# Causal mask by a matmul in PSUM and softmax normalisation by diagonal matrices in a two-block network on one core

## What is computed

```python
# MLA, 8 heads of 128+64: causal over blocks of 128 queries
sc = einsum('bqhd,bkhd->bhqk', qb, kb) * scale
p = softmax(where(mask, sc, -inf), axis=-1)
o = einsum('bhqk,bkhv->bqhv', p, vb)
# differential, 8 heads with two maps of width 64 each
p = softmax(where(mask, einsum('bqhid,bkhid->bhiqk', qb, kb) * scale, -inf), axis=-1)
a = p[:, :, 0] - lam * p[:, :, 1]
o = einsum('bhqk,bkhe->bqhe', a, vb)      # then an RMS norm per head
# cross attention, 4 heads of 256: softmax over 256 memory tokens, no mask
```

## Time and profile before

| | |
|---|---|
| median of 3 runs | 3108.59 us (3104.44 to 3113.85) |
| the profiled execution | 3112.86 us, its span 3111.0 us |
| PE busy | 2752.4 us (88%) |
| DVE busy | 1968.1 us (63%) |
| ACT busy | 1237.7 us (40%) |
| POOL busy | 1422.2 us (46%) |
| mean granted TensorE clock | 0.913 of 2.4 GHz |

### The profile page before, as it was taken

How to read it: one execution, slowest core, us unless ns; L and a number is a source line. 1 busy time by engine, 2 the same in 40 slices (tenths; PEclk the granted TensorE clock), 3 DMA queues, 4 the chain that set the end, 5 groups by cost and what they waited for, 6 DMA issues and landing times.

```text
span 3111.0 us, 49422 instructions
## 1 busy us (share of the span) xinstructions
PE 2752.4 (88%) x20583; PEld 2600.7 (84%) x20583; DVE 1968.1 (63%) x2280; ACT 1237.7 (40%) x1358; POOL 1422.2 (46%) x1126
## 2 busy tenths in 40 slices
PE   3998789999976999999789999999779979779797
PEld 3998679999965999998764999999669968468797
DVE  5657766676658666656766765766765454754553
ACT  2444444444444444434232444444444334334342
POOL 0890949579293692984730098494550000000000
PEclk7998989999987999999865999999889989789898
DMA  7765558667462675866620486675535535033452
GB/s 267 267 245 161 190 176 267 214 226 265 162 238 82 214 269 178 266 241 200 207 83 1 160 273 236 211 262 203 187 108 178 187 133 175 24 99 131 139 177 108
DMA packets 357173, 576.21 MB, mean 185 GB/s; under 512 B 22255, under 2 KB 297898, under 8 KB 356906
## 3 DMA queue, kind: packets, MB, share of 16 engines
q1 hardware_dynamic: 357034, 574.29, 54.2%
HBM read 573.20 MB, written 1.05 MB: 185 GB/s over the span
## 4 chain that ended last, share of the span: by engine, by line
PE 71%; DVE 13%; POOL 5%; ACT 4%; issue 4%; DMA 3%; SPq 1%; POOLq 0%; DVEq 0%; ACTq 0%
PE ps L1663 59%; PE ps L1716 3%; POOL mod_acc L647 3%; ACT whi L674 2%; PE ps L1722 1%; PE ps L2051 1%; POOL mod_w L642 1%; DVE wlo L1040 1%; DMA raw<-in_ffn_w_in_dram 1%; PE ps L2042 1%; DVE conv L1479 1%; PE ps L1773 1%; DVE z L1201 1%; DVE z L1179 1%; DMA raw<-in_ssm_w_in_dram 1%
## 5 line engine op out<-in xcount | busy, mean ns | idle before, releaser
L1040 DVE TENSOR_TENSOR wlo<-raw,whi 128x2048 fp32r<-128x2048 f32 x387 | 978.6, 2532 | 657.0 <-ACT whi L674 655.6
L1663 PE MATMUL ps<-H_hi,whi 128*128 128x256 f32 x3840 | 1099.4, 286 | 60.2 <-DVE conv L1479 21.8
L1663 PE MATMUL ps<-H_lo,whi 128*128 128x256 f32 x3840 | 1094.4, 285 | 0.0
L1663 PE MATMUL ps<-H_hi,wlo 128*128 128x256 f32 x3840 | 1094.0, 285 | 0.0
L674 ACT ACTIVATE whi<-raw 128x2048 fp32r<-128x2048 f32 (+1 forms) x402 | 759.9, 1892 | 645.6 <-DMA raw<-in_ffn_w_in_dram 259.7
L1663 PEld LDWEIGHTS ps<-H_hi,whi 128*128 128x128 f32 x3840 | 745.3, 194 | 68.6 <-issue 40.9
L647 POOL TENSOR_TENSOR mod_acc<-mod_acc,mod_w 128x512 f32<-128x512 f32 x450 | 793.0, 1788 | 0.0
L1663 PEld LDWEIGHTS ps<-H_lo,whi 128*128 128x128 f32 x3840 | 745.5, 194 | 0.2
L1663 PEld LDWEIGHTS ps<-H_hi,wlo 128*128 128x128 f32 x3840 | 745.1, 194 | 0.0
L1663 PE MATMUL ps<-A_hi,whi 128*128 (+1 forms) x1880 | 537.1, 286 | 21.0 <-DVE wlo L1040 21.0
L1663 PE MATMUL ps<-A_hi,wlo 128*128 (+1 forms) x1880 | 534.9, 285 | 0.0
(11 more groups left out here) (318 smaller groups left out, 2777.2 us busy)
## 6 DMA issues: line engine op xcount, KB each, us to landing
raw<-in_ffn_w_in_dram SPq DMA_DIRECT2D x176, 1024.0 KB, 5.3
mod_w<-in_w_mod_dram SPq DMA_DIRECT2D x180, 768.0 KB, 5.3
raw<-in_ffn_w_out_dram SPq DMA_DIRECT2D x88, 1024.0 KB, 4.8
raw<-in_w_gate_up_dram SPq DMA_DIRECT2D x22, 1024.0 KB, 5.1
raw<-in_ssm_w_in_dram SPq DMA_DIRECT2D x20, 1024.0 KB, 6.9
raw<-in_w_in_dram SPq DMA_DIRECT2D x14, 1024.0 KB, 5.1
raw<-in_diff_w_in_dram SPq DMA_DIRECT2D x12, 1024.0 KB, 7.7
raw<-in_w_down_dram SPq DMA_DIRECT2D x11, 1024.0 KB, 4.8
```

The costliest lines, as they stand in the source:

```text
L1040: tt(wlo[b % RAW][:, r], raw[b % RAW][:, r], whi[b % RAW][:, r].bitcast(F32), ALU.subtract).then_inc(w_lo, 1)
L1663: m = pe.matmul(out, l, r, start=first and i == 0, stop=last and i == 2, skip_group_check=rest)
```

## The change

In the kinds "mla" and "diff" the mask is added by PE: behind each tile's products, one more product of the identity with the mask's 128x128 triangle, both rounded to float32r (`unit`, `mask`), is accumulated on the 128 columns that hold the diagonal. DVE then reduces the scores in PSUM: one reduction for each tile, for both maps of "diff" at once. ACT takes the exponential from PSUM, and PE's scores of the head after the next wait for `exped` instead of `maxed`. In "mla", "diff" and "xatt" DVE stops after the reciprocal (in "diff" after the factor of the second map) and signals `summed`; a new ACT part `scales(h)` writes, for each map and tile, a diagonal matrix: the identity times the factor of each row (`diag`). PE's turning is no longer a transpose: it is a float32 product of `prob` as the stationary operand with the diagonal matrix as the moving one, which turns and scales at once; in "diff" the products of the two maps accumulate. ACT's order is now exps(i), scales(i-1), turned(i-2), rounded(i-4). In `act_init` two copies fill `unit` and `mask`. The dilated kind computes as before.

```diff
@@ ATT and SIGNALS
-ATT = ("scores", "maxed", "exped", "probs", "turned", "turned_out", "mixed", "mixed_out")
+ATT = ("scores", "maxed", "exped", "summed", "probs", "turned", "turned_out", "mixed", "mixed_out")
@@ scalar, attend
-                            src = ps[:, 4 + h % 2, a:b] if full else prob[:, h % 4, m * width + a:m * width + b]
+                            src = prob[:, h % 4, a:b] if kind == "dilated" else ps[:, score_bank(h, m, maps), a:b]
...
+                def scales(h):
+                    act.wait_ge(s["summed"], n["summed"] + h + 1)
+                    for x in range(2 * maps):
+                        i = nc.scalar.activation(diag[:, h % 2, x, :], ident, ACT.Copy, scale=stat[:, h % 4, 12 + x:13 + x])
+                    i.then_inc(s["probs"], 1)
...
+                    if 1 <= i <= heads and kind != "dilated":
+                        scales(i - 1)
@@ scalar, act_init
+                copy(unit[:, :], ident)
+                copy(mask[:, :], kc("causal", 0, P))
@@ vector, attend, maxima
-                    if h >= 4:
-                        dve.wait_ge(s["turned"], n["turned"] + h - 3)
...
-                        for m in range(maps):
-                            src = ps[:, score_bank(h, m, maps), 0:CW]
-                            mask = kc("causal") if kind != "dilated" else kc2("dil_add")
-                            link(tt(prob[:, b, m * CW:(m + 1) * CW], src, mask, ALU.add))
-                        for m in range(maps):
-                            for t, (x, y) in enumerate(tiles):
-                                i = nc.vector.tensor_reduce(stat[:, b, 2 * m + t:2 * m + t + 1], prob[:, b, m * CW + x:m * CW + y], AX, ALU.max)
+                        first = score_bank(h, 0, maps)
+                        for t, (x, y) in enumerate(tiles):
+                            top = stat[:, b, 0:2 * maps].rearrange("p (m t) -> p t m", m=maps)[:, t, :]
+                            i = nc.vector.tensor_reduce(top, ps[:, first:first + maps, x:y], AX, ALU.max)
@@ vector, attend, normal
+                    inverse = nc.vector.reciprocal(stat[:, b, 12:12 + 2 * maps], stat[:, b, 8:8 + 2 * maps])
+                    if kind in ("mla", "xatt"):
+                        inverse.then_inc(s["summed"], 1)
+                        return
+                    link(inverse)
                     if kind == "diff":
-                        link(ts(stat[:, b, 14:16], stat[:, b, 14:16], tiny[:, 0:1], None, ALU.mult))
+                        ts(stat[:, b, 14:16], stat[:, b, 14:16], tiny[:, 0:1], None, ALU.mult).then_inc(s["summed"], 1)
+                        return
...
-                    if kind == "diff":
-                        link(i)
-                        for t, (x, y) in enumerate(tiles):
-                            i = stt(prob[:, b, x:y], prob[:, b, CW + x:CW + y], stat[:, b, 14 + t:15 + t], prob[:, b, x:y],
-                                    ALU.mult, ALU.add)
@@ tensor, attend, scores
-                        pe.wait_ge(s["exped"] if full else s["maxed"], (n["exped"] if full else n["maxed"]) + h - 1)
+                        seen = "maxed" if kind == "dilated" else "exped"
+                        pe.wait_ge(s[seen], n[seen] + h - 1)
...
+                            if causal:
+                                m = pe.matmul(ps[:, b, o + keys - P:o + keys], unit[:, :], mask[:, :], start=False, stop=True,
+                                              skip_group_check=True)
@@ tensor, attend, turn
-                        m = pe.transpose(ps[:, turned_bank(h), b:b + P], prob[:, h % 4, a:a + P], ident)
+                        for x in range(maps):
+                            m = pe.matmul(ps[:, turned_bank(h), b:b + P], prob[:, h % 4, x * CW + a:x * CW + a + P], diag[:, h % 2, 2 * x + t, :],
+                                          start=x == 0, stop=x == maps - 1)
```

More of the change, by code:

```diff
@@ L179 @@
     "hyb": dict(rot=8, rot_out=8, kq=4, kq_out=4, ret=4, ret_out=4, fin_mean=2, fin_cent=2,
-                fin_sq=4, fin_sum=4, fin_std=4, fin_n=4, fin_hi=4, fin_lo=4, **{k: 8 for k in ATT}),
+                fin_sq=4, fin_sum=4, fin_std=4, fin_n=4, fin_hi=4, fin_lo=4, **{k: 8 for k in ATT if k != "summed"}),
     "mem": dict(mem_std=1, mem_n=1),
@@ L397, in program @@
         pick = at("pick", [P, 11], room(44), F32R)
+        unit, mask = at("unit", [P, P], room(4 * P), F32R), at("mask", [P, P], room(4 * P), F32R)
         std = at("std", [P, 2, S], room(8 * S))
@@ L428, in program @@
         probT = at("probT", [P, 2, 512], o_s1 + 4 * 12 * S)
+        diag = at("diag", [P, 2, 4, P], o_ah)
         stat = at("stat", [P, 4, 16], room(256))
@@ L1848, in attend @@
                 full = kind == "xatt"
+                causal = kind in ("mla", "diff")
+                maps = 2 if kind == "diff" else 1
                 def parts(h):
@@ L1878, in turn @@
                         pe.wait_ge(s["turned_out"], n["turned_out"] + h - 1)
-                    moves = ((0, 0), (128, 256), (256, 128), (384, 384)) if full else ((0, 0), (128, 128), (256, 256))
-                    for a, b in moves:
-                        m = pe.transpose(ps[:, turned_bank(h), b:b + P], prob[:, h % 4, a:a + P], ident)
+                    moves = ((0, 0, 0), (128, 256, 0), (256, 128, 1), (384, 384, 1)) if full else ((0, 0, 0), (128, 128, 1), (256, 256, 1))
+                    for a, b, t in moves:
+                        if kind == "dilated":
+                            m = pe.transpose(ps[:, turned_bank(h), b:b + P], prob[:, h % 4, a:a + P], ident)
+                            continue
+                        for x in range(maps):
+                            m = pe.matmul(ps[:, turned_bank(h), b:b + P], prob[:, h % 4, x * CW + a:x * CW + a + P], diag[:, h % 2, 2 * x + t, :],
+                                          start=x == 0, stop=x == maps - 1)
                     m.then_inc(s["turned"], 1)
```

8 lines of the change are left out of this document (7 added, 1 removed).

## The result

The changed kernel takes **3144.24 us** (median of 4 runs, 3139.51 to 3156.53), the kernel before 3106.52 beside it (4 runs, 3101.42 to 3113.85). The ratio is **1.0116**, 95% interval 1.0095 to 1.0137: slower by 37.7 us, where 15.7 us less were forecast. The profiled execution took 3148.21 us, span 3146.4 against 3111.0.

The account below looks back on a forecast made before the run. PE held 71% of the chain, but POOL bounded MLA, DVE the differential attention, PE the cross attention. Differential -17.7, cross +2.0 and MLA 0 sum to -15.7 us: 3092.9 from 3108.6, own bounds 3088 to 3100, with rivals 3083 to 3109.

Parts of the forecast that it names:

- The small multiplication L1332: Term of the differential attention's two-head loop: DVE's small multiplication after the maxima, priced at its mean, 0.65 us.
- DVE's wait in the other direction is plain: Sign cited for GpSimd holding up DVE: L1332 and L1344 average 0.65 and 0.83 us on two to four elements.
- Scores: Loop term in differential attention: score products of two maps on PE, one after the other, 1.29 us at 2.4 GHz.
- Masks: Loop term in differential attention: four single-pass 128-column products on PE at 0.10 us, 0.40 us; each between 0.06 and 0.215.
- Differential, -17.7: Differential attention: 4.36 us a head against 7.52 saves 15.8, the tail 2.4, normalisation loses 0.5: 17.7 us saved.
- MLA, 0: Both MLA stages: attention ends about 9 us sooner but none of it arrives; 0, -1 to +1 us each.
- The cover is POOL: MLA stages: POOL's modulation work sets the end, so PE comes sooner to L1773 and waits about 15 us instead of 6.
- Cross attention, +2.0: Cross attention: turning by fp32 products costs 1.7 us, the first head's wait 0.3; 2.0 us slower, 1.5 to 3.5.
- Opening step, 0: Opening step: two added ACT copies of at most 0.31 us fall into ACT's 4.45 us idle time; no change.
- Rival 1: MLA gains too: without DVE's scaling on the shared data path POOL's chain shortens, 5 us a stage; 3083 us; chance 0.10.
- Rival 2: Differential attention keeps the low clock, PE the bound at 7.3 us a head; 3109 us in total; chance 0.15.
- Rival 3: Low clock in all of these attentions: +6 us an MLA stage, cross attention +19; about 3138 us; chance 0.05.

Follow-up runs that it names:

- e1: Changed kernel with the small tensor_scalars of VectorE in MLA and differential attention moved to ScalarE or into a scaled identity made once: 3107.10 us, ratio 0.9987.
- e4: Changed kernel with GpSimd waiting for the end of each of its multiplies and adds before issuing the next: 3129.71 us, ratio 1.0061.
- e7: Changed kernel with unused 128x256 SBUF-to-SBUF tensor_scalars added on VectorE, one a head in MLA, two in differential: 3114.04 us, ratio 0.9995.
- e10: e9 with 36 unused products put on TensorE behind the V projection, ahead of the differential attention's first scores: 3093.74 us, ratio 0.9943.
- e8: e1 with a head's score products next to each other and its masks behind them; result wrong in the first query tile: 3088.21 us, ratio 0.9916.
- e11: e2 with a head's score products together, masks behind them, one start for a bank: 3040.09 us, ratio 0.9773.
- e12: Changed kernel with only the score order altered (products first, masks behind, one start for a bank), small operations left on VectorE: 3129.81 us, ratio 1.0066.
- e9: Changed kernel without small VectorE tensor_scalars in MLA and differential, masks behind all products, one start a bank, cross attention as before the change: 3088.40 us, ratio 0.9927.
- e6: Changed kernel without the mask matmul: VectorE adds the mask and reduces from SBUF as before, diagonals kept: 3157.32 us, ratio 1.0134.
- e2: Changed kernel with GpSimd's multiply and add cut to 8 of 1536 columns for every row block but the first: 3053.76 us, ratio 0.9823.

## Why the prediction was wrong

**The step that failed first: "The small multiplication L1332: 0.65, its mean now; bounds 0.4 and 0.9"**, and with it "DVE's L1344 (0.83) and the reciprocal lie beside ACT's exponentials". I took the mean of a wait as the price of an operation. It was a price under a condition, that VectorE also runs large SBUF-to-SBUF operations, and the change removes just these. In their place single operations took 15.19, 17.33 and 14.23 us. Shown by e1 (without them, 37.1 us less), e4 (with gaps at GpSimd, none over 1.24) and e7 (with large ones added, 30 us less). The prediction named the right rows as a sign, "DVE's wait in the other direction is plain", and looked only at how GpSimd would gain.

**The second: "Scores: ... two maps with one of each, 1.29" and "Masks: ... 0.40".** Together 1.69 us, at the upper level of the clock. The kernel after took 3.02 at a granted 0.94. With the products of the two maps adjacent e10 took 1.44 at full clock, 0.85 for the products, which then run side by side, and 0.59 for the masks. The forecast had counted no such overlap ("I take them one after the other"), so the loss of it is not what the sum lacks. Lacking is a term for the alternation itself: 3.02 - 1.69 = 1.33 us a head, by my estimate 0.17 for each of its eight changes between a 64-row and a 128-row product. In MLA a mask stands between the products as well, but all of them have 128 rows, and there a head's scores and masks take 1.48 us where the forecast's prices give 1.29 + 0.20 (e1, PE, granted clock 1.00 over 360 to 364 us):

```profile
361.28 0.39 PE L1891 MATMUL ps<-KN,QN 128*128 128x128 f32 x2
...
362.76 0.92 PE L1909 MATMUL ps<-diag,prob 128*128 128x128 f32 x6
```

That the order is the cause e8, e11 and e12 show: 7.9, 18.3 and 12.4 us of the differential stage. What TensorE does at such a change no run shows.

By its other steps:
- **Differential, -17.7**: it was +18.0. With both causes mended it is -16.9 (e9). The loop that the forecast described exists, two heads a round, at 7.97 us against its 8.72. Single terms at full clock in e9: turning 1.38 to 1.44 against 1.29, mixing 0.75 against 0.65.
- **MLA, 0**: it was +8.6 and +13.8. "The cover is POOL" held only while VectorE's own work was not late beyond it. Mended, it is -2.4 and -0.2, and there the cover is real, though it is partly VectorE's conversion and GpSimd holding each other up (12.48 and 6.24 us in e1) that keeps the gain away.
- **Cross attention, +2.0**: measured +2.4; the turning 0.89 us against 0.86, and four of these give 1.8 of it. The Trainium skill's factor of four for the transpose mode (TensorE: Matmul & The Clock Gate, Terms) would have given 5.3; here the ratio is 0.89 / 0.44, about two.
- **Opening step, 0**: its end is at 251.3 instead of 251.7 us.
- **Rival 1**, GpSimd's chain in MLA shortens: it did, the last addition ended at 388.3 instead of 396.0 us, and nothing came of it, because VectorE was held so much longer. Nor was it for the reason given. Six units took 34.9 us instead of 35.4 beside the attention, so VectorE's scaling had cost GpSimd 0.5 us and not 5. The forecast read only VectorE as the loser, but the trace before the change has GpSimd losing too, behind the attention, where VectorE's subtractions for the weights run (2.02 us is usual for these three):

```profile
378.11 6.18 POOL L642 TENSOR_SCALAR mod_w<-mod_w,cond 128x512 f32<-128x512 f32 x3
```

  This and a second one of 4.06 at 388.17 are 6.2 of the 7.7 us; after the change the subtractions come too late to hold it. The Trainium skill, SBUF — State Buffer (two separate sides), has whoever starts first hold the pair of ports for its whole instruction. The trace agrees that the loser stops, but adds that a loser can lose to one instruction after the other: the operation at 944.98 stood through about 20 of them.
- **Rival 2**, a low clock in the differential attention at 7.3 us a head: measured 6.80 once GpSimd was silent. Its size came true, but through another mechanism. The clock was 0.50 for most of the turning and into the mixing, and the scores were slow at 0.94. In e9, with more work per microsecond on PE, it was 0.96.
- **Rival 3**, slower, had the sign and nearly the size (3138), but not the cause: the MLA clock fell to 0.66 behind 370 us, where PE was waiting.

What would have found it: asking of every wait in the profile what ends it today, and whether the change touches that.

## What to carry to other kernels

A short wait in a profile is no constant: it belongs to the mix of instructions around it. Before taking large SBUF-to-SBUF operations from VectorE while GpSimd works without a pause, take the small ones away too, or move them to ScalarE; a kernel can get 30 us slower by losing work. And when products are added to TensorE, put them behind those that use half of its rows, not between them.

## What the runs showed of the hardware

- A VectorE tensor_scalar of 128x2, SBUF to SBUF, 0.17 us undisturbed, took up to 19.43 us (e6) beside GpSimd instructions of about 0.7 to 1.25 us issued back to back. With each of these waiting for the one before, the longest was 1.24 us, at 0.6 us more for a unit of seven.
- Reductions from PSUM and reciprocals on VectorE were never held in the same stretches (reciprocals 151 to 178 ns in the kernel after). A subtraction with two SBUF inputs was (12.48 us in e1), and such subtractions held GpSimd in turn: three of its multiplications, 2.02 us elsewhere, took 6.18 (before) and 6.24 (e1).
- Two maps' products of 64 rows (four products): 0.85 us at 2.4 GHz adjacent, 1.6 at 1.2 GHz. With a 128-row mask product after each: 3.02 at a granted 0.94, 5.36 at 0.50; the four masks take 0.6 and 1.04 when they stand together. Between products of 128 rows a mask cost no more than itself (MLA, 1.48 us a head).
- TensorE's granted clock went up and down within one head, 0.50 in the turning and about 1 in the interleaved scores, with PE busy throughout (e2: 0.50 at 910 to 912 us, 1.00 at 906 to 908). What decides it stays open.
